# Cached pages from the host in two layouts, no page transposes on chip, page products over three bank pairs

## The reference

```
x = x + 1/2 * SwiGLU_FFN1(rmsnorm(x))
h = rmsnorm(x);  P = h @ w_in -> [GLU input | q_a | c_kv | k_pe | gate_a | gate_b]
A: GLU -> causal depthwise conv (31) -> LayerNorm -> swish -> pointwise projection
B: latent attention: c = rmsnorm(c_kv), k_nope = W_uk c, rotary key k_pe shared by the 8 heads,
   per-head RMS norm over [nope | rope] of queries and keys, causal softmax, values W_uv c, projection
x = x + w_out( sigmoid(gate_a) * A + sigmoid(gate_b) * B )
x = x + 1/2 * SwiGLU_FFN2(rmsnorm(x))
```

## Time and profile before

| | |
|---|---|
| median of 3 runs | 1528.22 us (1528.05 to 1530.12) |
| profiled execution, its own time | 1529.87 us |
| its span | 1528.0 us |
| DVE, ACT, POOL busy | 1055.5, 659.7, 448.2 us |
| moved by DMA | 122.82 MB, 80 GB/s |
| transposes of latent pages (L1760) | 256, of 0.27 us each, partly on top of each other |
| page products (L1868) | 1536 |

### The profile page before, as it was taken

The page is one execution under the profiler, slowest core; times in us unless marked ns, Lnnn a source line. Parts: engine busy times, 40 slices in busy tenths (PEclk is TensorE's granted clock), DMA queues, the critical chain, the costliest instruction groups (busy, mean ns, idle before and its releaser), DMA issues.

```text
span 1528.0 us, 31401 instructions
## 1 busy us (share of the span) xinstructions
PE 1513.9 (99%) x11059; PEld 1463.9 (96%) x11059; DVE 1055.5 (69%) x1738; ACT 659.7 (43%) x1247; POOL 448.2 (29%) x463
## 2 busy tenths in 40 slices
PE   8999999999999999999999999999999999999999
PEld 8999999999999999588999999988999999999999
DVE  6999898422269975865877787864659998985000
ACT  6444445322221241364666666662434544444111
POOL 4000002454455743320233333223551000005432
PEclk9999999999999999999999999999999999999999
DMA  6233334232323571002322222312222333332322
GB/s 176 70 97 98 94 90 123 66 95 76 82 75 96 94 119 48 1 1 61 76 67 60 66 63 63 89 56 71 83 82 67 99 96 89 103 95 80 90 76 82
DMA packets 239316, 122.82 MB, mean 80 GB/s; under 512 B 37041, under 2 KB 236146, under 8 KB 239218
## 3 DMA queue, kind: packets, MB, share of 16 engines
q1 hardware_dynamic: 238354, 121.09, 29.6%
q10 hardware_dynamic: 864, 0.48, 0.1%
HBM read 117.95 MB, written 3.58 MB: 80 GB/s over the span
## 4 chain that ended last, share of the span: by engine, by line
PE 67%; issue 21%; POOL 7%; DVE 2%; ACT 2%; DMA 1%; SPq 0%; POOLq 0%; ACTq 0%; DVEq 0%
PE ps L490 29%; PE ps L1506 14%; PE ps L1868 11%; POOL w_lobuf L465 7%; PE ps L1760 1%; PE ps L1631 1%; PE ps L1685 1%; PE ps L1660 1%; PE ps L1799 1%; PE ps L1778 1%; PE ps L1828 1%; PE ps L1779 1%; DMA w_rawbuf<-in_ffn_w_gu 1%; PE ps L476 1%; PE ps L1675 1%
## 5 line engine op out<-in xcount | busy, mean ns | idle before, releaser
L465 POOL TENSOR_TENSOR w_lobuf<-w_rawbuf,w_hibuf 128x256 fp32r<-128x256 f32 (+1 forms) x328 | 316.9, 997 | 798.7 <-ACT w_hibuf L458 798.5
L1506 PE MATMUL ps<-xs,w 128*128 128x288 f32 x3192 | 427.4, 296 | 0.8 <-DVE w L1994 0.8
L1506 PEld LDWEIGHTS ps<-xs,w 128*128 128x128 f32 x3192 | 426.8, 188 | 1.3 <-issue 1.3
L458 ACT ACTIVATE w_hibuf<-w_rawbuf 128x1024 fp32r<-128x1024 f32 (+1 forms) x89 | 104.4, 1172 | 348.1 <-PE ps L490 332.9
L2202 DVE SCALAR_TENSOR_TENSOR xT<-ps,xT 128x576 f32<-128x576 f32 x23 | 17.4, 757 | 202.4 <-PE ps L490 202.4
L1994 DVE TENSOR_TENSOR w<-w_raw,w 128x512 fp32r<-128x512 f32 x228 | 153.5, 688 | 1.0 <-ACT w L1006 0.8
L490 PE MATMUL ps<-a_hi,w_lobuf 128*128 128x288 f32 x682 | 147.5, 297 | 0.0
L490 PE MATMUL ps<-x_hi,w_hibuf 128*128 128x288 f32 x656 | 142.6, 299 | 4.6 <-POOL w_lobuf L465 2.7
L490 PE MATMUL ps<-a_hi,w_hibuf 128*128 128x288 f32 x682 | 147.2, 296 | 0.0
L490 PE MATMUL ps<-a_lo,w_hibuf 128*128 128x288 f32 x682 | 145.4, 294 | 0.0
L490 PE MATMUL ps<-x_lo,w_hibuf 128*128 128x288 f32 x656 | 141.3, 297 | 0.0
(11 more groups left out here) (343 smaller groups left out, 2729.6 us busy)
## 6 DMA issues: line engine op xcount, KB each, us to landing
w_raw<-in_ffn_w_gu SPq DMA_DIRECT2D x76, 256.0 KB, 2.9
up_rows<-in_ffn_w_gu SPq DMA_DIRECT2D x72, 256.0 KB, 3.1
c_nat<-in_cache_ckv SPq DMA_DIRECT2D x128, 128.0 KB, 2.0
w_rawbuf<-in_w_in SPq DMA_DIRECT2D x58, 256.0 KB, 3.2
w_rawbuf<-in_ffn_w_down SPq DMA_DIRECT2D x32, 384.0 KB, 4.1
w_rawbuf<-in_ffn_w_down SPq DMA_DIRECT2D x32, 320.0 KB, 3.4
w_rawbuf<-in_ffn_w_gu SPq DMA_DIRECT2D x24, 256.0 KB, 3.4
w_rawbuf<-in_w_out SPq DMA_DIRECT2D x16, 256.0 KB, 3.2
```

The source lines that it names most:

```text
L458: act.activation(w_hibuf[:, r % HIS, 0:size], w_rawbuf[:, r, 0:size], ACT.Copy).then_inc(w_hi_done, 1)
L465: ins = pool.tensor_tensor(w_lobuf[:, r, part], w_rawbuf[:, r, part], w_hibuf[:, r % HIS, part].bitcast(F32), ALU.subtract)
L1506: mm = pe.matmul(ps[:, seven_bank(f, slot), 0:HALF], m, xs[:, slot, n, k, :], start=k == 0 and j == 0, stop=k == KH - 1 and j == 2)
```

## The change

The host lays out the cache in three arrays beside the kernel's other inputs: `pages_t` (each latent page transposed, as two 128x128 halves side by side), `pages_in` (latent and rotary columns together, 128x288) and `pages_k` (rotary keys transposed, 32x128). On the chip:

- `transpose_pair`, `kpe_transpose` and ACT's `kpe_copy` go.
- SP loads transposed pages into a ring of eight (`c_ring`), transposed keys straight into `kpeT`, and natural rows with rotary columns into `c_nat`, which grows to 288 columns. A group is four index loads, then four ring pages behind a wait for the low parts of the group before the last, four key blocks behind a wait for that group's rotary scores, and four natural pages behind `pages_used`.
- ACT's and DVE's split of a pair reads the ring in SBUF, not PSUM; ACT waits for the transfer and for the products of the pair before the last.
- Page products rotate over bank pairs 2-3, 4-5 and 0-1, with page 15 on 4-5.
- `c_lo` of all pairs is written over `c_nat`; the separate `c_lo_first` goes. POOL squares the rotary columns in place. Some small tiles move.
- In front, ring group 0 and its keys are loaded before the prologue's last waits. Behind, `w_uv` is loaded after the first two merge weights and after the last low part.

```diff
-def layer(nc, x_t, cols_in, cache_ckv, cache_kpe, state_conv, page_table, w, const, out):
+def layer(nc, x_t, cols_in, pages_t, pages_in, pages_k, state_conv, page_table, w, const, out):
...
-        c_nat = place("c_nat", [P, 2, NP, KL], F32, A0)
...
-        kpe_nat = place("kpe_nat", [P, 2, NP, DR], F32, S3)
+        c_nat = place("c_nat", [P, 2, NP, KL + DR], F32, A0)
+        assert 8 * NP * (KL + DR) <= S1 - A0
...
+        RING = 8
+        c_ring = place("c_ring", [P, RING, KL], F32, S3)
...
-        o_lat = place("o_lat", [P, KL + 2], F32, A0 + 35552)
...
+        o_lat = place("o_lat", [P, KL + 2], F32, causal_at)
...
-        c_lo_first = place("c_lo_first", [P, NP // 4, KL], F32R, S3 + 4096)
...
         def page_banks(t):

-            return 2 + 2 * (t % 2)
+            return 4 if t == NP - 1 else (2, 4, 0)[t % 3]
+
+        def banks_free(t):
+
+            return {0: -3, 1: 0, 2: -1, NP - 1: NP - 2}.get(t, t - 2)
...
             def page_of(s, t):
-                return sp.value_load(pages[0:1, ds(s * NP + t, 1)], min_val=0, max_val=cache_ckv.shape[1] - 1)
-
-            def load_page(src, dst, landed, page, b, t):
-                sp.dma_start(dst[:, b, t, :], src[0, ds(page, 1), :, :].rearrange("a p c -> (a p) c")).then_inc(landed[b][t // 4], 16)
-
-            def load_pages(s, b, used=None, split=None):
+                return sp.value_load(pages[0:1, ds(s * NP + t, 1)], min_val=0, max_val=pages_t.shape[0] - 1)
+
+            def load_ring(g, found):
+
+                for u, page in enumerate(found):
+                    sp.dma_start(c_ring[:, (4 * g + u + RING // 2) % RING, :], pages_t[ds(page, 1), :, :].rearrange("a p c -> (a p) c"))\
+                        .then_inc(ring_in[g % 2], 16)
+
+            def load_rows(b, g, found):
+
+                for u, page in enumerate(found):
+                    sp.dma_start(c_nat[:, b, 4 * g + u, :], pages_in[ds(page, 1), :, :].rearrange("a p c -> (a p) c")).then_inc(nat_in[b][g], 16)
+
+            def load_kpe(g, found):
+
+                for u, page in enumerate(found):
+                    sp.dma_start(kpeT[u * DR:(u + 1) * DR, g % 2, :], pages_k[ds(page, 1), :, :].rearrange("a d t -> (a d) t")).then_inc(kpe_in[g % 2], 16)
+
+            def load_pages(s, b, used=None):
+
                 for g in range(NP // 4):
-                    if used is not None and g == 0:
-                        sp.wait_ge(split_made, split)
-                    elif used is not None:
+                    found = [page_of(s, 4 * g + u) for u in range(4)]
+                    sp.wait_ge(ct_lo, s * PAIRS + (2 * g - 2))
+                    load_ring(g, found)
+                    sp.wait_ge(pe_scored, s * (NP // 4) + (g - 1))
+                    load_kpe(g, found)
+                    if used is not None:
                         sp.wait_ge(pages_used, used + 2 * (g + 1))
-                    for t in range(4 * g, 4 * g + 4):
-                        page = page_of(s, t)
-                        load_page(cache_ckv, c_nat, ckv_in, page, b, t)
-                        load_page(cache_kpe, kpe_nat, kpe_in, page, b, t)
-
-            AHEAD = 11
+                    load_rows(b, g, found)
+
+            sp.wait_ge(rows_done, 2 * NT + PT_TILES)
+            found = [page_of(0, u) for u in range(4)]
+            load_ring(0, found)
+            load_kpe(0, found)
...
             sp.wait_ge(prep_q, 1)
-            for t in range(AHEAD):
-                load_page(cache_ckv, c_nat, ckv_in, page_of(0, t), 0, t)
+            load_rows(0, 0, found)
+            for g in (1, 2):
+                load_rows(0, g, [page_of(0, 4 * g + u) for u in range(4)])
...
+            found = [page_of(0, 4 + u) for u in range(4)]
+            load_ring(1, found)
+            load_kpe(1, found)
+            load_rows(0, 3, [page_of(0, 12 + u) for u in range(4)])
+            for g in (2, 3):
+                found = [page_of(0, 4 * g + u) for u in range(4)]
+                sp.wait_ge(ct_lo, 2 * g - 2)
+                load_ring(g, found)
+                sp.wait_ge(pe_scored, g - 1)
+                load_kpe(g, found)
             sp.wait_ge(prep_mm, 2)
             load_pages(1, 1)
             with sp.Fori(1, NS // 2) as i:
                 for b in range(2):
-                    load_pages(i * 2 + b, b, i * (2 * PAIRS) + (EARLY_PAIRS + PAIRS * (b - 2)), i * (2 * SPLITS) + (SPLITS * (b - 2) + 2))
+                    load_pages(i * 2 + b, b, i * (2 * PAIRS) + (EARLY_PAIRS + PAIRS * (b - 2)))

             sp.wait_ge(lat_mm, STACKED)
-            sp.dma_start(w_uv[:, :, :], w["w_uv"][0].rearrange("(k p) h d -> p k (h d)", p=P)).then_inc(late_in, 16)
             for t in range(2):
                 load_merge(t)
+            sp.wait_ge(ct_lo, NS * PAIRS)
+            sp.dma_start(w_uv[:, :, :], w["w_uv"][0].rearrange("(k p) h d -> p k (h d)", p=P)).then_inc(late_in, 16)
             sp.wait_ge(page_mm, NS * NP)
             sp.wait_ge(pe_scored, NS * (NP // 4))
             for t in range(2, KD):
...
                 two = slice(2 * j, 2 * j + 2)
                 pool.wait_ge(p_done, high_made(r, j))
-                pool.tensor_tensor(c_lo_first[:, two, :] if j < 2 else c_lo[:, b, two, :], c_nat[:, b, two, :],
+                pool.tensor_tensor(c_lo[:, b, two, 0:KL], c_nat[:, b, two, 0:KL],
                                    c_hi[j % EARLY_PAIRS][:, :, 0:KL].bitcast(F32), ALU.subtract)\
                     .then_inc(split_made, 1)
...
                 for g in range(NP // 4):
-                    pool.wait_ge(kpe_in[b][g], landed_pages(g, uses))
-                if prev:
-                    pool.wait_ge(kpe_red, s)
-                k = kpe_nat[:, b].rearrange("p t d -> p (t d)")
-                pool.tensor_tensor(ta[:, 0:NP * DR], k, k, ALU.mult).then_inc(kpe_sq, 1)
+                    pool.wait_ge(nat_in[b][g], uses * 64)
+                k = c_nat[:, b, :, KL:KL + DR]
+                pool.tensor_tensor(k, k, k, ALU.mult).then_inc(kpe_sq, 1)
...
-            def pages_hi(n, b):
-
-                act.wait_ge(ct_tr, n + 1)
-                act.activation(cT_hi[:, b, :], ps[:, b, :], ACT.Copy).then_inc(ct_hi, 1)
+            def pages_hi(s, pp):
+
+                act.wait_ge(ring_in[pp // 2 % 2], (s * 2 + (pp // 4 + 1)) * 64)
+                if not (isinstance(s, int) and s == 0 and pp < 2):
+                    act.wait_ge(page_mm, s * NP + (2 * pp - 2))
+                act.activation(cT_hi[:, pp % 2, :], ring_pair(pp), ACT.Copy).then_inc(ct_hi, 1)
...
-            def pair_high(r, b, j):
-
-                act.wait_ge(ct_tr, r * PAIRS + (j + 1))
+            def pair_high(r, b, j, uses):
+
+                act.wait_ge(nat_in[b][j // 2], uses * 64)
                 act.wait_ge(pages_used, r * PAIRS + (j + 1))
-                act.activation(c_hi[j % EARLY_PAIRS][:, :, 0:KL], c_nat[:, b, 2 * j:2 * j + 2, :], ACT.Copy).then_inc(p_done, 1)
-
-            def kpe_copy(s, g):
-
-                act.wait_ge(pe_tr, s * 4 + (g + 1))
-                if not (isinstance(s, int) and s == 0 and g < 2):
-                    act.wait_ge(pe_scored, s * 4 + (g - 1))
-                act.activation(kpeT[:, g % 2, :], ps[:, PEB, 4 * HQ:4 * HQ + P], ACT.Copy).then_inc(pe_copied, 1)
+                act.activation(c_hi[j % EARLY_PAIRS][:, :, 0:KL], c_nat[:, b, 2 * j:2 * j + 2, 0:KL], ACT.Copy).then_inc(p_done, 1)

             def act_seq(s, b, uses, prev, nxt):
                 soft = soft_act(s - 1, 1 - b) if prev else None
...
-            def transpose_pair(s, b, uses, pp):
-
-                n = s * (NP // 2) + pp
-                if pp % 2 == 0:
-                    pe.wait_ge(ckv_in[b][pp // 2], landed_pages(pp // 2, uses))
-                if not (isinstance(s, int) and s == 0 and pp < 2):
-                    pe.wait_ge(ct_lo, n - 1)
-                for u in range(2):
-                    for k in range(2):
-                        c = (2 * u + k) * P
-                        tr = pe.transpose(ps[:, pp % 2, c:c + P], c_nat[:, b, 2 * pp + u, k * P:(k + 1) * P], ident[:, :])
-                tr.then_inc(ct_tr, 1)
-
             def soft_pe(r, b):
...
-            def kpe_transpose(s, b, g, uses):
-
-                pe.wait_ge(kpe_in[b][g], landed_pages(g, uses))
+            def kpe_scores(s, g):
+
+                pe.wait_ge(kpe_in[g % 2], (s * 2 + (g // 2 + 1)) * 64)
                 if isinstance(s, int) and s == 0 and g == 0:
                     pe.wait_ge(prep_copied, 2)
-                if not (isinstance(s, int) and s == 0 and g == 0):
+                else:
                     pe.wait_ge(scores_read, s * 4 + g)
-                pe.transpose(ps[:, PEB, 4 * HQ:4 * HQ + P], kpe_nat[:, b, 4 * g:4 * g + 4, :].rearrange("p t d -> p (t d)"), ident[:, :])\
-                    .then_inc(pe_tr, 1)
-
-            def kpe_scores(s, g):
-
-                pe.wait_ge(pe_copied, s * 4 + (g + 1))
```

(50 more changed lines are left out.)

34 lines of the change are left out of this document (14 added, 20 removed).

## The result

| | median of 7 runs | range |
|---|---|---|
| before | 1529.65 us | 1528.05 to 1532.78 |
| changed | 1538.76 us | 1535.72 to 1540.88 |

The changed kernel is slightly slower, clear of the noise: ratio 1.0057, 95% interval 1.0047 to 1.0066. The profiled execution has a span of 1536.8 us, 8.8 more than before. The forecast was 1515 us, with a range from 1499 to 1527.

A forecast was written before the change was run, and what follows sets the result against it. PE, busy 99%, bounds the kernel before; afterwards SP's loads set the pace from sequence 1. Savings of 13.0 us took 1529.9 to 1516.9, and 1.65 for the median gave 1515.2, said as 1515; range 1499 to 1527.

The forecast's parts named there:

- PE work removed: Page stage on PE: transposes and slower first products gone, 0.89 us a group, 28.5 us over 32 groups.
- ACT, DVE, POOL: Page splits: new SBUF sources put at nothing, -0.5 to +0.5 us a sequence; 29 us of DVE fits in 33.6.
- SP, the part that decides: SP's load queue: 9.15 us a group, 36.6 us a sequence, more than PE's 33.6, so SP sets the pace; 0.63.
- Blocking hidden by SP's pace: DVE's low splits beside POOL: 1.6 us of DVE hidden; rival: 1.5 us at two late groups, 1525 us, chance 0.09.
- The sum, by its terms: Savings listed for the start and each sequence, together 13.0 us off the profiled execution's 1529.9.
- the stall of ACT for the merge weights: Sequence 7: ACT stands still up to 10 us, PE's 7.1 us hide most, so about 0 saved (-2 to +2).
- SP hidden: Rival on SP's queue: four index loads overlap, 7.1 us a group, full PE gain, 1499 us; chance 0.14.
- SP costs much more: Rival on SP's queue: dearer transfers, from 9.6 us a group; at 10.0 us a group 1539 us; chance 0.14.

The follow-up runs named there:

- e1: The changed kernel with one page index load a group instead of four, all transfers and waits kept: 1531.0 us, 1.0008 of before.
- e3: The changed kernel with ACT making the seventh pair's high part ahead of the second half of the exponentials: 1531.7 us, 1.0014 of before.
- e10: The kernel before with two new orders: seventh pair's high part ahead of the second exponentials, latents' copy first: 1527.9 us, 0.9988 of before.
- e9: The changed kernel with SP's loop written out, seventh pair's high part ahead of exponentials, latents' copy first, third pair's ahead of the root: 1513.4 us.
- e5: The changed kernel with SP's loop written out, seventh pair's high part ahead of exponentials, POOL's late low parts 8 columns wide: 1513.7 us.
- e6: The changed kernel with SP's loop written out, seventh pair's high part ahead of exponentials, DVE's copy of the latents first: 1515.7 us.
- e7: The changed kernel with page products back on two pairs of PSUM banks: 1535.9 us, 1.0038 of before.

## Why the prediction was wrong

- **PE work removed: right.** 33.6 to 33.9 us busy in sequences 1 and 2, and 29.0 us less work in the stage at a full clock.
- **"ACT, DVE, POOL" at nothing: the first step that failed.** I checked that 29 us of DVE fit into 33.6, a sum. What decides is the order in it. The trace of before held the row: the seventh pair's low part was ready 0.2 us ahead of PE. A stretch in which PE is never idle can still be exactly as long as the chain beside it; taking work out of it then buys idle time. Shown by e1 (37.16 us a sequence with SP free), e3 and e10. This join holds 12.2 of the 30.1 us of waits; 10.0 more are 18 small ones ahead of other pairs, of which e9 took some. The estimate for DVE's new source, at most 0.5 us a sequence, was also short: DVE is 2.1 to 2.7 us busier in sequences 1 and 4 (31.78 against 29.12, 31.32 against 29.16).
- **"SP, the part that decides": the second step that failed.** The price of an undisturbed group was right, 9.0 us where 9.05 were worked out. The mean was not: 9.66 instead of 9.15, and 9.62 in e3, where SP waits for nobody. I had no term for the loop's edge, 2.9 us, and 0.1 a group for slow issues, which cost 8 us in 23 steps. By the sum's own measure, 2.8 us for each 0.1, that alone takes 13 to 14 us, the whole gain, and e3, in which SP sets the pace, came to 1531.7. In the changed kernel itself relieving SP gives back 7.5 us only (e1), because the chain ahead of page 12 then holds 37.16 us a sequence.
- **Blocking hidden by SP's pace: wrong.** It lay on the path to the latents' copy (e5); the rival's mechanism held and its size of 1.5 us a group did not.
- **No term for the clock: wrong.** Sequences 3 to 7 lost 10.5 us to it. Each fall stood behind an idle time of PE, and e6 and e10, with little idle, have none in the sequences; but e7's profile has none either, with idle times up to 2.5 us, and e5's has one behind 2.9 us at 766. No run took the two apart: that the idle brings the falls is argued, not shown.
- **The sum, by its terms** (saved, forecast against the windows): start and sequence 0 4.4 and 2.8; sequence 1 1.7 and 0.3; 2 to 4 2.0 and -4.1; 5 3.2 and -2.7; 6 1.7 and -0.4; 7 0 and -4.5. Sequence 5 has three waits of 1.5 to 2.2 us, each at another join. In 7 the stall of ACT for the merge weights came as described, 4.75 us, but PE's latent products did not hide all of it: the sum of the denominators behind it held PE 2.2 us, and the clock fell:

```profile
1006.35 1.06 ACT L461 ACTIVATE w_hibuf<-w_rawbuf 128x1024 fp32r<-128x1024 f32 x1 [4.75 <-DMA w_rawbuf<-in_w_conv_out]
```

- **The rivals.** "SP hidden", 1499, was twice wrong. The four index loads do not overlap (SP's 2.85 us between rows and ring pages are four times 0.65 and the wait, and three fewer save 2.3 in e1). The Trainium skill's remark on unrolling loads by four ("DMA: Bandwidth & Descriptors", Latency and other measured facts), read as an overlap, is not borne out for register loads written side by side, each with its bounds check. And with SP hidden in fact, e1 came to 1531. "SP costs much more", 1539, has the right time, and the mean of 9.66 us a group passed the 9.6 from which it was to decide. But the twelve transfers kept their price where nothing disturbed them, and 1539 came about by the joins and the clock beside SP, not by 10 us a group: that the number agrees is in part luck.

## What to carry to other kernels

Before taking work off the busiest engine, look at each of its joins for how long ahead the other side was ready; where that is 0.2 us, the work is filling a chain, and its removal gives little until the order of the chain is changed. Price an engine's loop by its mean, with the back edge and the slow issues in it, not by an undisturbed pass. An engine that takes its queue in order must not meet a transfer for later ahead of a step that somebody waits for now. And try single repairs together: here 3.7 and 6.6 us made 15.1, and 7.5 and 6.6 made 19.3.

## What the hardware showed that I had not expected

- The back edge of SP's loop over eight groups cost 2.9 us. Written out, with constant addresses, a group took 8.4 instead of 8.9 to 9.0 us.
- A DVE subtraction of two SBUF operands took 1.59 us beside POOL and 0.68 alone; with one operand in PSUM never over 0.70 in 64.
- In the changed kernel the granted clock fell behind idle times of 1.6 to 2.3 us of PE, five times in eight sequences (0.54 to 0.74 in the lowest window of 4 us), and not behind others of 2.1 to 2.7 us.
- Three index loads fewer made an undisturbed group of SP 2.3 us shorter (e1): loads side by side ran one after another.
